# Feed forwards of a two-block transformer kernel: gate and up pairs as seven block products, weight sums by accumulating DMAs

## What is computed

```python
def swiglu_ffn(x, w_gate, w_up, w_down):
    return (jax.nn.silu(x @ w_gate) * (x @ w_up)) @ w_down

def second_block(x, ...):
        x = x + 0.5 * swiglu_ffn(rmsnorm(x, ffn1_norm[l]), ffn1_w_gate[l], ffn1_w_up[l], ffn1_w_down[l])
        x = x + hybrid_mixer(rmsnorm(x, mix_norm[l]), ...)
        x = x + 0.5 * swiglu_ffn(rmsnorm(x, ffn2_norm[l]), ffn2_w_gate[l], ffn2_w_up[l], ffn2_w_down[l])
        x = rmsnorm(x, final_norm[l])
```

## Time and profile before

| | us |
|---|---|
| median of 3 runs | 1785.98 |
| lowest and highest run | 1784.14, 1787.6 |
| the profiled execution's span | 1785.5 |
| feed forward 1, from the first matmul of cut (0, 1) to that of part 2's down projection | 938.4 to 1212.4 |

### The profile page before, as it was taken

The page is one execution under the profiler, slowest core; times in us unless marked ns, Lnnn a source line. Parts: engine busy times, 40 slices in busy tenths (PEclk is TensorE's granted clock), DMA queues, the critical chain, the costliest instruction groups (busy, mean ns, idle before and its releaser), DMA issues.

```text
span 1785.5 us, 20614 instructions
## 1 busy us (share of the span) xinstructions
PE 1748.2 (98%) x8607; PEld 1284.3 (72%) x8607; DVE 923.1 (52%) x1339; ACT 603.3 (34%) x938; POOL 12.5 (1%) x22
## 2 busy tenths in 40 slices
PE   7999999998999999999999999999999999999998
PEld 6878888875454544544478888888877888888886
DVE  5768865643333333333444745635578535736634
ACT  4556335442111111111233323324355433423322
POOL 0000000000000000000000000000000000000000
PEclk9999999998999999999999999999999999999999
DMA  6222225547999999999832242233321232241331
GB/s 219 90 71 72 95 83 177 192 161 288 422 421 421 421 421 421 420 421 421 340 114 71 72 141 71 91 122 98 115 71 37 80 133 71 71 159 54 108 104 59
DMA packets 93315, 331.16 MB, mean 185 GB/s; under 512 B 6192, under 2 KB 15552, under 8 KB 68512
## 3 DMA queue, kind: packets, MB, share of 16 engines
q1 hardware_dynamic: 88928, 318.33, 46.8%
q0 software_dynamic: 1984, 7.25, 1.2%
q10 hardware_dynamic: 2304, 4.20, 0.6%
HBM read 323.46 MB, written 6.29 MB: 185 GB/s over the span
## 4 chain that ended last, share of the span: by engine, by line
PE 91%; DVE 5%; ACT 3%; DMA 0%; issue 0%; SPq 0%; DVEq 0%; ACTq 0%
PE PS L1427 12%; PE PS L1557 11%; PE PS L1559 10%; PE PS L1558 10%; PE PS L1460 6%; PE PS L1553 5%; PE PS L1555 5%; PE PS L1554 5%; PE PS L1527 3%; PE PS L1528 3%; PE PS L1526 3%; PE PS L1398 2%; PE PS L1470 2%; PE PS L1399 2%; PE PS L1631 2%; PE PS L1471 2%
## 5 line engine op out<-in xcount | busy, mean ns | idle before, releaser
L2271 DVE TENSOR_TENSOR lo<-raw,hi 128x1024 fp32r<-128x1024 f32 (+2 forms) x147 | 250.4, 1709 | 318.7 <-ACT hi L1862 315.5
L1862 ACT CAST hi<-raw 128x1024 fp32r<-128x1024 f32 (+2 forms) x149 | 214.2, 1446 | 297.9 <-PE PS L1559 111.9
L1557 PE MATMUL PS<-xh_ffn,hi 128*128 128x512 f32 x576 | 225.0, 391 | 0.0
L1559 PE MATMUL PS<-xh_ffn,lo 128*128 128x512 f32 x576 | 224.3, 389 | 0.0
L1558 PE MATMUL PS<-xl_ffn,hi 128*128 128x512 f32 x576 | 224.2, 389 | 0.0
L1559 PEld LDWEIGHTS PS<-xh_ffn,lo 128*128 128x128 f32 x576 | 108.1, 188 | 22.6
L1558 PEld LDWEIGHTS PS<-xl_ffn,hi 128*128 128x128 f32 x576 | 108.2, 188 | 22.2
L1557 PEld LDWEIGHTS PS<-xh_ffn,hi 128*128 128x128 f32 x576 | 108.2, 188 | 22.2
L1427 PE MATMUL PS<-raw,XG 128*64 128x512 f32 x352 | 117.1, 593 | 0.0
L2231 DVE TENSOR_TENSOR HF<-SG,PS 128x512 f32<-128x512 f32 x16 | 17.4, 1090 | 165.0 <-PE PS L1427 165.0
L2246 DVE SCALAR_TENSOR_TENSOR YL<-PS,SM,YH 128x512 fp32r<-128x512 f32 x30 | 21.1, 746 | 138.8 <-ACT YH L1845 138.8
(11 more groups left out here) (510 smaller groups left out, 3678.3 us busy)
## 6 DMA issues: line engine op xcount, KB each, us to landing
raw<-in_w_in SPq DMA_DIRECT2D x26, 1024.0 KB, 5.2
rawz<-in_w_down_experts SPq DMA_DIRECT2D x25, 1024.0 KB, 10.1
raw<-in_w_up_experts SPq DMA_DIRECT2D x24, 1024.0 KB, 14.8
raw<-in_w_gate_experts SPq DMA_DIRECT2D x20, 1024.0 KB, 15.0
raw<-in_ffn_w_down SPq DMA_DIRECT2D x20, 1024.0 KB, 5.0
rawz<-in_w_up_experts SPq DMA_DIRECT2D x19, 1024.0 KB, 18.8
raw<-in_w_down_experts SPq DMA_DIRECT2D x16, 1024.0 KB, 11.5
rawz<-in_w_gate_experts SPq DMA_DIRECT2D x16, 1024.0 KB, 13.1
```

The source lines that it names most:

```text
L1557: e.matmul(o, h[:, kk, c], xh[:, k, :], start=s0, stop=False)
L1559: x = e.matmul(o, l[:, kk, c], xh[:, k, :], start=False, stop=s1)
L1862: e.copy(q.hi[:, a:b], q.raw[:, a:b]).then_inc(*a_hi((u, 0) if part == 0 else u))
L2271: e.tensor_tensor(q.lo[:, a:b], q.raw[:, a:b], q.hi[:, a:b].bitcast(F32), ALU.subtract).then_inc(*v_lo(key))
```

## The change

Five of the six cuts of gate and up ((0,1), (1,0), (1,1), (2,0), (2,1)) are computed as seven block products, as the down projections were: the left matrix is x in 2 token halves x 2 halves of its 1024 columns, the right one has the halves of w_gate's and w_up's rows as its four blocks. Results have tokens on the partitions. A class `Four` holds the units of one set of four blocks; its plan is the order t3, b11, b21, t2, t1, b22, t4, one unit for one product of 24 matmuls. `SETS` gives the order: gu (0,1), s 0, gu (1,0), gu (1,1), s 1, gu (2,0), gu (2,1), where s is a down projection. No gate products stand between those of an s set any more. The hidden values of all cuts are now turned by PE (`turn_hidden` for every cut: 4 token blocks, 4 or 3 transposes each), copied by ACT into `HF8`, and the left operands of the down products are made from there. PSUM banks: products 0 and 6 use banks 4 and 5, products 1, 3, 4 and 5 banks 0 and 1, product 2 banks 2 and 3; a product on a bank in use continues its sum, once ACT (R1, R2, R4) has copied the value so far (in s sets: once DVE has added it to x_sb).

The four sums of weight blocks are made no longer by DVE but by DMAs issued from POOL which add their source onto a raw buffer (`onto`, `accum_op=ALU.add`): T3 = t3's block plus b22's from memory, T2 = T3 plus b11's from memory, T1 = b11 plus t3's from memory, T4 = b21 plus the raw buffer of T2. POOL waits for the `lo` of the unit in that buffer, and for T4 also for T2. ACT's `rounded` waits for the DMA's semaphore. There is a fifth raw buffer (`raw5`), and a planner `place_ffn` which gives each load the buffer that comes free first.

At the start of each feed forward DVE adds hi and lo of x back together (`whole`) and makes S1 to S4 of x. FNB, PI and the norm row "n2" move to other places in memory or time. The diff, cut:

```diff
@@ -187,40 +187,59 @@
 FPARTS = [[(0, 512), (512, 1024)], [(1024, 1536), (1536, 2048)], [(2048, 2432), (2432, 2816)]]
 NS = 2
 
-SEVEN = ("P1", "P2", "P6", "P7", "P4", "P5", "P3")
-MADE = {2: "T2", 3: "T3", 4: "T4", 5: "T1"}
-QUARTER = [(0, 0), (0, 0), (0, 1), (1, 1), (1, 0), (1, 1), (0, 1)]
+
+class Four:
+
+
+    def __init__(self, key, w11, w12, w21, w22, n):
+        def unit(src, made=None):
+            q = Unit(key, src, 4, n)
+            q.four, q.made = self, made
+            return q
+
+        self.key = key
+        self.t3, self.b11, self.b21, self.b22 = unit(w12, "T3"), unit(w11), unit(w21), unit(w22)
+        self.t2, self.t1, self.t4 = (unit(None, t) for t in ("T2", "T1", "T4"))
+        self.loads = [self.t3, self.b11, self.b21, self.b22]
+        self.plan = [self.t3, self.b11, self.b21, self.t2, self.t1, self.b22, self.t4]
+
+
+SEVEN = ("S3", "A11", "A12", "S2", "S1", "S4", "A22")
+BANK = (4, 0, 2, 0, 0, 0, 4)
+PAST = {3: 1, 4: 3, 5: 4, 6: 0}
+QUARTER = [(1, 1), (0, 0), (0, 0), (1, 0), (1, 1), (0, 1), (1, 0)]
+SETS = [("gu", 0, 1), ("s", 0), ("gu", 1, 0), ("gu", 1, 1), ("s", 1), ("gu", 2, 0), ("gu", 2, 1)]
 
 
 def make_plan_ffn(I, pre):
-    plan, loads = [], []
+    plan, loads, fours = [], [], {}
     wg, wu, wd = (I[f"{pre}_w_{n}_2"][0] for n in ("gate", "up", "down"))
+
+    def rows(w, k, a, b):
+        return w[k * 128:k * 128 + 512, a:b].rearrange("(k p) n -> p k n", p=128)
...
-            g0, g1 = units((pre, "g", p + 1, 0), wg, 0, 8, *FPARTS[p + 1][0])
-            plan.extend([b11, b21, t2, b12, t4, g0, t1, g1, b22])
-            loads.extend([b12, b22, b11, b21, g0, g1])
+    for w, m in (("g", wg), ("u", wu)):
+        both((pre, w, 0, 0), m, 0, 8, *FPARTS[0][0])
+    for what in SETS:
+        key = (pre, *what)
+        if what[0] == "gu":
+            a, b = FPARTS[what[1]][what[2]]
+            q = Four(key, rows(wg, 0, a, b), rows(wu, 0, a, b), rows(wg, 4, a, b), rows(wu, 4, a, b), b - a)
         else:
-            for c in range(2):
-                both((pre, "d", p, c), wd, r // 128, cuts[1][1] // 128, c * 512, c * 512 + 512)
-    return plan, loads
+            k = FPARTS[what[1]][0][0] // 128
+            q = Four(key, rows(wd, k, 0, 512), rows(wd, k, 512, 1024), rows(wd, k + 4, 0, 512), rows(wd, k + 4, 512, 1024), 512)
+        fours[key] = q
+        plan.extend(q.plan)
+        loads.extend(q.loads)
+    p = len(FPARTS) - 1
+    for c in range(2):
+        both((pre, "d", p, c), wd, FPARTS[p][0][0] // 128, FPARTS[p][1][1] // 128, c * 512, c * 512 + 512)
+    return plan, loads, fours
 
 
 INP = [("qa", 0, 512), ("kv", 512, 768), ("qh", 768, 1280), ("fh", 1280, 1792), ("gh", 2304, 2816), ("ih", 1792, 2304),
...
@@ -640,24 +659,73 @@
 
 def schedule_ffn(S, feed, pre, order, name):
     first_gate_ffn(S, feed, pre, order)
-    dense(S, feed, (pre, "u", 0, 0), 2, 4, order)
-    for p, cuts in enumerate(FPARTS):
-        for cut, (a, b) in enumerate(cuts):
-            for w in "gu":
-                if cut == 0 and (p == 0 or w == "g" and p <= NS):
-                    continue
-                for j, _ in enumerate(dense_steps(S, feed, (pre, w, p, cut), 2, (b - a) // 128)):
-                    if (w, p, cut) == ("g", 0, 1) and j < 4:
-                        S.append(("turn_hidden", pre, j, 4 + j))
-                    if p < NS and cut:
-                        for at, step in (("g", 5), ("sum", "S3")), (("g", 6), ("sum_lo", "S3")), (("u", 0), ("made", "T3")), \
-                                (("u", 1), ("made", "T2")):
-                            if at == (w, j):
-                                S.append((step[0], pre, p, step[1]))
-        if p < NS:
-            schedule_seven(S, feed, pre, p)
+    key = (pre, "u", 0, 0)
+    for ui in range(2):
+        u = feed.take(key)
+        for j, i in enumerate(range(4) if ui else order):
+            S.append(("mm", key, ui, i, u))
+            if ui:
+                S.append(("ev", key, i))
+            elif j == 1:
+                S.extend([("whole", pre, 0), ("whole", pre, 1)])
+            elif j == 2:
+                S.extend([("sum", pre, "x", "S3")] + split_left(pre, "x", "S3"))
+
+    def turns(p, cut, blocks):
+        return [("turn_hidden", pre, p, cut, tb, 6 + tb % 2) for tb in blocks]
+
+    past = None
+    for what in SETS:
+        behind = {j: [] for j in range(7)}
+        ahead = []
+        if past:
+            ahead = turns(*past, (0, 1))
+            behind[0] = [(w, pre, *past, t) for w in ("sgb", "hb") for t in range(2)]
+        if what[0] == "gu":
+            p, cut = what[1:]
+            own = {1: ("R1",), 2: ("C11",), 3: ("sg", "R2"), 4: ("R4", "C22"), 5: ("ht",), 6: ("C21",)}
+            for j, ws in own.items():
+                behind[j].extend((w, pre, p, cut, t) for w in ws for t in range(2))
+            if past:
+                behind[0].extend(turns(*past, (2, 3)))
+            if (p, cut) == (0, 1):
+                behind[0].extend([("sum", pre, "x", "S1"), ("sum", pre, "x", "S2")] + split_left(pre, "x", "S2"))
+                behind[1].extend(split_left(pre, "x", "S1") + [("sum", pre, "x", "S4")])
+                behind[2].extend(split_left(pre, "x", "S4") + turns(0, 0, (0, 1)))
+                behind[3].extend(turns(0, 0, (2, 3)))
+            if p < NS and cut:
+                j = 2 if p else 4
+                behind[j].extend([("sum", pre, p, "S3")] + split_left(pre, p, "S3"))
+                behind[j + 1].extend(split_left(pre, p, "A11"))
+            past = (p, cut)
+        else:
+            p = what[1]
+            behind[0].extend(split_left(pre, p, "A12") + turns(*past, (2, 3)))
+            behind[1].extend([("sum", pre, p, "S1"), ("sum", pre, p, "S2")] + split_left(pre, p, "S2"))
+            behind[2].extend(split_left(pre, p, "S1"))
+            behind[3].append(("sum", pre, p, "S4"))
+            behind[4].extend(split_left(pre, p, "S4"))
+            behind[5].extend(split_left(pre, p, "A22"))
+            for j, js in ((1, (1,)), (2, (0,)), (3, (3,)), (4, (4,)), (5, (5, 2)), (6, (6,))):
+                behind[j].extend(("seven_x", pre, p, q, t) for q in js for t in range(2))
+            past = None
+        for j in range(7):
+            u = feed.take((pre, *what))
+            S.extend(ahead if j == 0 else ())
+            S.extend(("seven", (pre, *what), j, t, u) for t in range(2))
+            S.extend(behind[j])
     p = len(FPARTS) - 1
-    dense(S, feed, (pre, "d", p, 0), 2, 4)
+    key = (pre, "d", p, 0)
+    for ui in range(2):
+        u = feed.take(key)
+        if ui == 0:
...
@@ -1370,7 +1397,38 @@
...
+            def onto(t, src, key, f):
+                dst = t.raw[:, 0:4 * t.n]
+                e.dma_start(dst.rearrange("p (k n) -> p k n", k=4) if t is not f.b21 else dst, src, accum_op=ALU.add).then_inc(*d_T[key](f.key))
+
+            def first_sum(f):
+                pool.wait_ge(d_w[f.t3.slot], U.index(f.t3))
+                onto(f.t3, f.b22.src, "T3", f)
+
+            def seven(key, j, t, u):
+                f = fours[key]
+                nxt = SETS.index(key[1:]) + 1
+                if t:
+                    return
+                if j == 0:
+                    if nxt == 1:
+                        first_sum(f)
+                    pool.wait_ge(v_lo, U.index(f.t3))
+                    onto(f.t3, f.b11.src, "T2", f)
+                elif j == 1:
+                    pool.wait_ge(v_lo, U.index(f.b11))
+                    onto(f.b11, f.t3.src, "T1", f)
+                elif j == 2:
+                    pool.wait_ge(v_lo, U.index(f.b21))
+                    pool.wait_ge(d_T["T2"], key)
+                    onto(f.b21, f.t3.raw[:, 0:4 * f.t3.n], "T4", f)
+                    if nxt < len(SETS):
+                        first_sum(fours[(key[0], *SETS[nxt])])
+                elif j == 6 and key == ("ffn1", "s", 1):
+                    pool.wait_ge(v_sum, ("S3l", "ffn1", 1))
+                    row("n2")
...
@@ -1500,34 +1558,47 @@
...
+            def seven(key, j, t, u):
                 q = U[u]
-                b = 4 + t if pr in (1, 5, 6) else 6 + t
-                h, l = (x[:, 0:2048].rearrange("p (k n) -> p k n", k=4) for x in (q.hi, q.lo))
-                xh, xl = LEFT[pr]
+                b = BANK[j] + t
+                h, l = (x[:, 0:4 * q.n].rearrange("p (k n) -> p k n", k=4) for x in (q.hi, q.lo))
+                xh, xl = (LEFT_H if key[1] == "s" else LEFT_X)[j]
                 pe.wait_ge(a_hi, u)
                 pe.wait_ge(v_lo, u)
-                if pr < 2:
+                more = j in PAST
+                if not more:
                     taken(b)
+                elif key[1] == "s":
+                    pe.wait_ge(v_sum, ("x", key[0], key[2], PAST[j], t))
+                elif j == 6:
+                    pe.wait_ge(v_ev, ("C22", *at_set(key), t))
                 else:
-                    pe.wait_ge(v_sum, ("x", n, p, {2: 0, 3: 2, 4: 3, 5: 1, 6: 5}[pr], t))
```

(74 more changed lines are left out.)

387 lines of the change are left out of this document (154 added, 233 removed).

## The result

The changed kernel takes 1791.67 us (median, 1787.16 to 1793.43) beside 1785.61 us for the kernel before on the same chip. The ratio is 1.0031, 95% interval 1.0024 to 1.0039: slower by 0.3%. Forecast were 1781.2 us, faster by 0.3%, so the prediction had the wrong sign, although its range (1768 to 1845) holds the time. Its chances were nearly even, 0.39 for faster and 0.40 for slower, but the 0.40 stood for rivals A, C and D. The execution profiled for the changed kernel is the longest of its sixteen timed ones (1793.43).

A forecast was written before the change was run, and what follows sets the result against it. PE's streaming was taken to bound the stage. Per feed forward, 15.1 us saved on PE less 12.7 of new waits gave -2.4, two -4.8, additions hidden: 1781.2 us, range 1768 to 1845.

The forecast's parts named there:

- rival A: Weight-sum additions land late and their queue sets the pace: 1859 us at 12 us each, 2015 at 15; chance 0.20.
- C: More waits than set out: hops 0.5 us longer at 24 products with little slack, 1805 us; chance 0.15.
- Rival D: PE's 384-column matmuls cost 0.188 us each, its weight load, in place of 0.1734: 1791 us; chance 0.05.
- What PE loses and gains: PE per feed forward: 23.3 us less for matmuls, 8.2 more for transposes, net 15.1 saved if nothing waits.
- both ends fitted a straight line: PE's pace for 384 columns, 0.1734 us, read between 0.120 for 256 and 0.2268 for 512.
- Waits: PE's waits on ACT's and DVE's small steps in the seven-product sets: 12.7 us a feed forward, allowance -6 and +8.
- signs that the prediction named for being wrong: ACT's hi waiting for weight sums, 384-column starts not near 0.17, or PE's waits under 7 or over 20 us a feed forward.
- rival B: ACT and DVE keep up because roundings overlap more, so PE has no waits: -30.2 us, 1755.8; chance 0.10.
- The sum: Per feed forward -15.1 + 12.7 = -2.4 us, -4.8 for two, giving 1781.2 us.
- The additions: Accumulating DMAs on POOL's queue, one after the other, are hidden if they land in time, costing nothing.
- 8.0 taken: Landing time assumed for one accumulating DMA, in us, from POOL's pair of 1 MB transfers issued together.
- the rule: Additions in a row, L us each: T1 needs 2 L - 1.1 up to 18.3, T3 4 L - 1.1 up to 35; L up to 9.0 free.

The follow-up runs named there:

- after: The changed kernel itself, compared with the kernel before: 1791.67 us, ratio 1.0031; its profiled execution took 1793.43 us.
- all_order: Changed kernel with the first T3 addition issued early and ACT's and DVE's small steps reordered in s, gate and up sets: 1759.67 us.
- filled2: Changed kernel with seven short runs of useless matmuls per feed forward put where PE waits: 1787.12 us, ratio 1.0013.
- add_plain: Kernel with the early T3 and all reorderings, its accumulating DMAs overwriting in place of adding: 1760.31 us, ratio 0.9859.
- add_serial: Kernel with the early T3 and all reorderings, GpSimd waiting for each addition to land before issuing the next: 1815.89 us, ratio 1.0173.
- filled: Changed kernel meant to run useless matmuls in PE's waits; they never ran in the feed forwards, so a second measurement of it: 1790.48 us.
- t3_early: Changed kernel with feed forward 1's first weight sum (T3) issued ahead of GpSimd's wait for gate products and small loads: 1787.88 us.
- s_order: Changed kernel with another order of ACT's and DVE's small steps in the s sets alone: 1775.13 us, ratio 0.9946.
- gu_order: Changed kernel with another order of the small steps in the gate and up sets alone: 1779.14 us, ratio 0.9965.

## Why the prediction was wrong

**What PE loses and gains: right.** Matmuls of 384 columns start 0.173 us apart (forecast 0.1734). That both ends fitted a straight line was no evidence, since any two points do; the measured distance is. Twelve distances in after, from 1169.37 to 1171.45:

```profile
1169.37 0.33 PE L1594 MATMUL PS<-hi,XS2h 128*128 128x384 f32 x1
...
1171.45 0.33 PE L1594 MATMUL PS<-hi,xh_ffn 128*128 128x384 f32 x1
```

Rival D is out, although its 1791 us is nearest to the time measured: a coincidence. Without losses a feed forward would be 15.2 us shorter (forecast 15.1), and all_order realises 13.2 of them.

**Waits: right in sum and nearly in place.** Forecast 12.7 us a feed forward, measured 13.5 and 12.4 by starts. Place by place, in listed idle time: product 6 of gu (0,1) 2.36 (2.5), product 4 of gu (1,1) 1.74 (1.9), product 3 of the s sets 2.15 (2.2), x_sb 0.77 (0.8) at product 5 in the three s sets where a slow stretch follows product 3's wait, and 0.59 at product 4, the place forecast, in the one where none does. Product 2 of gu (0,1) waits 1.16 (1.2) in the second feed forward; in the first the 2.08 at product 0, for the crowded addition, stands in its place. That one was not foreseen, since the working let the first T3 land in good time and did not look at what else uses the DMA engines then; ACT's hi waited 3.24 us for a weight sum there, one of the signs that the prediction named for being wrong. So rivals B and C are out: the queue layout from the durations of the earlier trace rows held to 0.2 us. What rival B said could be had by a small reordering, all_order got: 1759.67 us beside B's 1755.8.

**The sum: the step that failed.** It was -15.1 + 12.7, as if a wait cost only its own length. A term was missing: what PE's clock does behind the wait. PE had no wait at all in this stage before and a clock of 1.00, so nothing there priced it; the one dip of the clock in the earlier trace rows, an 8 in the slice from 402 to 446 us, was not looked into, and the term stood at nothing without a reason. In the profiled execution the term is 6.66 + 1.68 = 8.3 us. The account of the 10.8 us between -4.8 and +6.0 there (the 6.1 above, less rounded): clock in the feed forwards 8.3; waits 0.5 (25.9 against 25.4); small rests 2.5; 1.4 in the mixer; less 0.2 more ideal saving and less 1.7 at the span's start, where before happened to run longer at the lower clock.

In the timed runs the median missed the forecast by 10.5 us, and the clock is only 3 to 5 of them. At the usual clock of before the kernel would stand near 1787, by its one run there and by filled2, within 0.2% of before and still not ahead of it: the missing term made "same" into "slower", but it did not turn "faster" into "same" alone. The small rests and the mixer, which the sum put at nothing, are 3.9 us in the profile; what else keeps the timed runs above 1781.2 stays open. With 3 to 5 us for the clock in its sum, "same" would have been the likeliest case.

**The additions (rival A): right that they are hidden, for a wrong reason.** Landings of 8.2 to 9.8 us for 1 MB, and 10.4 to 16.4 for T3, against 8.0 taken and a limit of 9.0 by the rule. The 8.0 itself was the median of four single transfers; issued in pairs, the two of a pair were through 9.7 and 11.3 us after the first issue. By that rule the changed kernel would have been at its edge; it wasn't, because GpSimd doesn't wait for one to land before the next, and in all_order they land before ACT rounds them: 1.7 us before at the tightest (T1 of gu (2,0): issued 1139.51, landed 1146.75, rounded 1148.44), not the 3.8 that the expectation of add_plain gives, and mostly 3 to 11. The rule also left out T3's 15 us beside plain loads and the rounding that closes the loop; add_serial shows what that is worth, 56 us. Had the additions run one after the other, something like rival A would have come true, at single additions of about the length that the prediction took. The Trainium skill's "Collectives: The Full Stack", section "The bandwidth ceiling: the fold count and why AG ≠ RS ≠ AR", gives half the rate of a copy for an operation that reads two sources; 58.5% against 30.1% of engine time agrees.

**The mixer.** 1.4 us more between the feed forwards: PE has one new wait of 1.4 us, up to 1362.32, for a copy `v` by ACT. That copy starts at 1361.68, behind two roundings of weights of 1.90 us each (from 1357.59 and from 1359.88). The variants have it too (179.4 to 180.3 us against 178.06). Whether it stands there because the list of units grew was not tried.

**The start.** The 1.7 us by which the first feed forward starts earlier are the clock among the experts, as shown above: in the profiles of the variants it starts at 886.3 to 888.2, and later the longer PE ran at the lower clock before.

## What to carry to other kernels

When a change takes work off a PE that never waits and puts small waits in its place, each wait has two prices: its length and the slow matmuls that can follow. Count the waits one by one, not only their sum: here a wait of 2.1 to 2.4 us was worth up to 1.7 us more than its length. Where a neighbour engine is busy for only part of the time (DVE 67% here) and still late, its in-order queue is the suspect: moving the rounding that PE needs next ahead of the sums and copies that nobody needs yet was worth 28 us, and with one addition issued early 32, five times what the change itself had lost. For DMAs that run one behind another, work out the whole loop, with the crowded one at its crowded length and the engines that close it.

## What the runs showed of the hardware

- An accumulating DMA of 1 MB from GpSimd's queue into SBUF lands mostly in 8.3 to 8.7 us alone when its source is in memory and in 6.9 to 7.0 when it is in SBUF (add_serial), a plain one on the same queue in 5.2 to 5.6 (median, add_plain); for the same bytes it uses 1.94 times the DMA engine time. Beside two plain loads it lands in 13 to 15 us, in the crowded start in 16.4. A quarter of it lands in 3.3 to 4.2 alone.
- Issuing it takes GpSimd 0.87 to 1.65 us, a plain one 0.55 to 0.76.
- After a wait of 2.1 to 2.4 us PE ran eight or nine matmuls at 0.43 us in place of 0.23, in five of seven cases in one execution, and at the same place in one feed forward but not in the other. In the profiles of after, filled, t3_early, s_order and gu_order together, 16 of the 27 waits of 1.85 to 2.4 us in the feed forwards had such a stretch behind them, and none of the shorter ones, up to 1.75 us, had. In add_serial each of the seven waits of 3.3 us and more had one.
- A kernel's own spread is largely the clock: the changed kernel's sixteen runs go from 1787.2 us at a mean clock of 0.995 to 1793.4 at 0.990. The kernel before, run beside the variants, goes from 1783.8 to 1784.6 at 0.996 over 1785.2 to 1786.3 at 0.995 to 1787.5 at 0.994.
- Matmuls of 512, 384 and 256 columns start 0.227, 0.173 and 0.120 us apart at the upper clock.
